# A hybrid diffusion step on one core: an eighth slot for expert weights, and attention queries scaled by ScalarE

## The chip, the cores and the metric

One NeuronCore of a Trainium2 chip runs the whole program. Its engines work side by side and wait for each other through semaphores: TensorE (PE) multiplies matrices into PSUM banks, VectorE (DVE) and ScalarE (ACT) read them out, GpSimd (POOL) helps with elementwise work, and SyncE (SP) issues most of the DMA transfers that bring weights from HBM into SBUF. The metric is the time of one execution in microseconds (us); a kernel is given by the median of its runs.

## The reference

Two layers act on 384 tokens of width 1024 (128 context tokens, 256 latent tokens). Everything is 32-bit. Each layer:

```
h   = rms_norm(x) * (1 + scale1) + shift1          # scale, shift, gate: from the conditioning vector
A   = grouped-query attention, 8 heads of 64, q and k RMS-normalised per head, rotary positions
B   = latent attention, 8 heads of 64 + 32, low-rank keys and values
C   = bidirectional gated linear recurrence (chunk scan)
x  += gate1 * ((sum over A, B, C of sigmoid(g_n) * (branch_n @ w_branch_n)) @ w_out)
h   = rms_norm(x) * (1 + scale2) + shift2
x  += gate2 * moe(h)                                # 16 experts, 2 per token, width 512
```

Attention is `softmax(q @ k.T * scale) @ v`, with `scale = 64 ** -0.5` in A and `96 ** -0.5` in B. Each expert has three weight matrices of 2 MB: gate, up and down.

## The kernel before, in words

**Slabs.** All large weights come as slabs of 128 x 4096 floats (2 MB). `slab_order()` lists them in the order in which they are loaded; `slab_slots()` gives each one a place. There are four ring slots (`sb_slabs`, slots 0 to 3) for everything, and three extra slots (slots 4 to 6, a part of `sb_arena` that the mixers no longer need at the end of a layer) for expert slabs alone. A slab takes the slot whose old slab is done with first. SP walks through the list: for each slab it waits until the slot's old slab has been read, then issues the load (L2088). The queue is in order, so a waiting load holds up all that follow. The slabs `eg`, `eu` and `ed` are an expert's gate, up and down matrices; `m` slabs are parts of the conditioning matrix, `o0` and `o1` the output projection, `br2` the third branch's projection.

**The mixer part of a layer.** PE computes the projections slab by slab. Attention runs over 24 units per layer: 2 mixers x 4 pairs of heads x 3 query tiles. The first tile of a pair sees 128 keys, the other two see 384. Per unit and head, `scores` (PE, L982) fills a bank, `maxima` (DVE) takes the row maximum negated (L1816) and multiplies it by the scale (L1817), `exps` (ACT, L1539) takes exp(scale * score - max) with its row sum, `softmax` (DVE, L1824 and L1826) divides, `turn` (PE, L1224) transposes, `probs_turned` (ACT, L1549) copies to SBUF, `values` (PE, L1241) multiplies by v, and `outputs` (DVE, L1832) copies the result to `oBr`, the branch outputs. PE's order is scores of unit s, turn of unit s - 1, values of unit s - 2. The queries come out of PSUM by ACT copies in `split` (mixer A, which also takes the squares for the head norm) and at L1512 (mixer B). After attention come the recurrence, the merge of the three branches (the last merge matmuls carry the key `("p", l, 2, j)`), the output projection, the second norm and the routing.

**The experts.** With at most 64 tokens per expert, the short path runs (`pe_short`, `act_short`, `dve_short`). Experts go in 8 pairs. For pair p, PE gathers the tokens by a matmul with a 0/1 matrix `pick` (L531), computes gate and up (L560, 32 matmuls each, one slab per expert and matrix), transposes (L570), and computes down of the pair before (L589). DVE tells SP by the semaphores `read_eg`, `read_eu` and `read_ed` (L754) when a pair's slabs have been read: two slots come free at a time. The rows of pairs 0 to 5 go through `yg` and an indirect DMA of GpSimd (L2059) to a buffer in HBM, `ybuf`; when all have landed, ACT's queue reads the buffer back in three parts (L691), ACT and DVE add a token's two rows (L697, L820), and PE transposes the sum back (L641). Pairs 6 and 7 are added by matmuls (L611). The down matmuls of pair 7 come after that transpose in PE's order.

`arena` holds, one after the other, the norm's scratch and `hT` (the normalised tokens, offsets 0 to 4224), the branch outputs `oBr` (from `o0` = 4224, 4608 long) and a region. During the experts, `hg`, `actT` and `ag` lie over the first part, `yg` and `pick` over the branch outputs. `tmp` (3072 long) holds squares and scratch of the norms and is free during the short expert path.

Of the kernel before, what the change touches and what calls it, by code (L numbers as in the profile page):

```python
# [27 lines left out]
D = 1024  # L28
# [29 lines left out]
RING = 4  # L58
EXTRA = 3
EXTRA_AT = 6144  # L60
GATES = 2
# [56 lines left out]
def slab_slots(order):  # L118

    index = {(l, n): i for i, (l, n, _) in enumerate(order)}
    ends = [index[l, f"g{n[2]}1"] if n[:2] == "br" else
            index[l, EXPERT_SLABS[EXTRA]] - 1 + (EXPERT_SLABS.index(n) + 1) / NE if n in AHEAD.values() else i for i, (l, n, _) in enumerate(order)]
    holds, times, out = [None] * (RING + EXTRA), [0] * (RING + EXTRA), []
    for i in range(len(order)):
        s = min(range(RING + EXTRA if order[i][1][0] == "e" else RING), key=lambda s: -1 if holds[s] is None else ends[holds[s]])
        times[s] += 1
        out.append((s, times[s], holds[s]))  # L130
        holds[s] = i
    return out
# [20 lines left out]
def program(nc, A, known):  # L153
# [5 lines left out]
    with ExitStack() as ctx:  # L159
# [14 lines left out]
        def signal(name, key):  # L174

            tally.next(name, key)
            return sem(name), 1
# [159 lines left out]
        hg = arena[:, 0:KT * 2 * SLOTS].rearrange("p (k n) -> p k n", k=KT)  # L337
        actT = arena[:, 2048:2048 + FT * 2 * SLOTS].rearrange("p (f n) -> p f n", f=FT)
        ag = arena[:, 3072:3072 + FE]
        yg = arena[:, o0:o0 + 2 * D].rearrange("p (b d) -> p b d", b=2)  # L340
        pick = arena[:, o0 + 2 * D:o0 + 2 * D + 3 * TT * 2 * SLOTS].rearrange("p (b t n) -> p b t n", b=3, t=TT)
        back = arena[:, KT * 2 * SLOTS:KT * 2 * SLOTS + 2 * T].rearrange("p (b t) -> p b t", b=2)
        extra = region[:, EXTRA_AT:EXTRA_AT + EXTRA * SLAB].rearrange("p (s n) -> p s n", s=EXTRA)
        ybuf = [nc.dram_tensor(f"ybuf{l}", (2 * T, D), F32).ap() for l in range(DEPTH)]

# [8 lines left out]
        dma_ytok = [[sem(f"dma_ytok{l}{t}") for t in range(TT)] for l in range(DEPTH)]  # L354
        dma_slab = [sem(f"dma_slab{i}") for i in range(RING + EXTRA)]
        outs = [0]

        def place(slot):
            return slabs[:, slot, :] if slot < RING else extra[:, slot - RING, :]

# [1061 lines left out]
        def _(sc):  # L1422
# [25 lines left out]

            def split(bkey, dst, sq, key, l, i, wait=None):

                sc.wait_ge(*full(bkey))
                ps = held(bkey)
                if wait:
                    wait()
                nc.scalar.activation(sq, ps[:, 0:T], ACT.Square).then_inc(*signal("square", (key, l, i)))
                nc.scalar.activation(dst, ps[:, 0:T], ACT.Copy).then_inc(*frees(bkey))

# [20 lines left out]
            for l in range(DEPTH):  # L1478
# [3 lines left out]
                for c in range(BT):  # L1482
                    split(("qa", l, c), qA[:, c, :], tmp[:, c, :], f"qa{c}", l, 0)
                for c in range(BT - 1):
# [24 lines left out]
                for h in range(HEADS):  # L1509
                    sc.wait_ge(*full(("qb", l, h)))  # L1510
                    ps = held(("qb", l, h))
                    nc.scalar.activation(qB[0:QB_W, h, :], ps[0:QB_W, 0:T], ACT.Copy).then_inc(*frees(("qb", l, h)))  # L1512
                if l == 0:
                    first_copy(NEXT + 1)
                for hp in range(HEADS // 2):
                    sc.wait_ge(*full(("kb", l, hp)))
                    ps = held(("kb", l, hp))
                    nc.scalar.activation(keysB[0:NOPE, 2 * hp, :], ps[0:HD, :], ACT.Copy).then_inc(*signal("kb_part", (l, hp)))
                    nc.scalar.activation(keysB[0:NOPE, 2 * hp + 1, :], ps[HD:P, :], ACT.Copy).then_inc(*frees(("kb", l, hp)))
# [7 lines left out]
                def exps(u):  # L1527
                    br, hp, qt = units[u]
                    c0, c1 = key_cols(qt)
                    for i in range(2):  # L1530
# [6 lines left out]
                        if u >= 2:  # L1537
                            sc.wait_ge(*full(("t", l, u - 2, i)))
                        nc.scalar.activation(probs[:, u % 2, i, 0:c1 - c0], ps[:, 0:c1 - c0], ACT.Exp, bias=nmx[:, u % 2, i:i + 1],  # L1539
                                                   scale=(SCALE_A, SCALE_B)[br], accum_out=rsum[:, u % 2, i:i + 1]).then_inc(*frees(("s", l, u, i)))  # L1540

# [120 lines left out]
        def _(ve):  # L1662
# [112 lines left out]
            for l in range(DEPTH):  # L1775
# [32 lines left out]
                def maxima(u):  # L1808
                    br, hp, qt = units[u]
                    c0, c1 = key_cols(qt)  # L1810
                    for i in range(2):
                        ve.wait_ge(*full(("s", l, u, i)))
                        ps = held(("s", l, u, i))
                        if u >= 2:
                            ve.wait_ge(*freed_by(("s", l, u - 2, i)))
                        step(V.tensor_reduce(nmx[:, u % 2, i:i + 1], ps[:, 0:c1 - c0], AX, ALU.max, negate=True))  # L1816
                        V.tensor_scalar(nmx[:, u % 2, i:i + 1], nmx[:, u % 2, i:i + 1], (SCALE_A, SCALE_B)[br], None, ALU.mult).then_inc(*signal("negmax", (l, u, i)))  # L1817

# [245 lines left out]
        def _(sp):  # L2064
# [3 lines left out]
            for i, (l, name, size) in enumerate(order):  # L2068
# [15 lines left out]
                if name == EXPERT_SLABS[EXTRA - 1]:  # L2084
                    sp.wait_ge(dma_out, 16 * (5 * l + 5))
                if l and i == index_of[l, "kv"] + 1:
                    sp.wait_ge(*made("x_ready", (l, 1, KT - 1)))
# [163 lines left out]
```

## Time and profile before

| what | value |
|---|---|
| median of 3 runs | 1878.6 us (1877.42 to 1880.3) |
| profiled execution: its time, its span | 1875.93 us, 1874.0 us |
| PE busy in the span | 1696.2 us (91%) |
| DVE, ACT, POOL busy | 945.3, 358.9, 353.7 us |
| mean granted TensorE clock | 0.955 |
| moved by DMA | 361.53 MB |

The span runs from the first to the last instruction that the profiler saw. Busy shares are averages over stages with different limits: a stage is read by the wait that ends last in it. The experts of layer 0 run from about 704 to 958 us, those of layer 1 from about 1606 to 1862 us; the attention units run from about 156 to 225 us and from about 1066 to 1136 us.

### The profile page before, as it was taken

The numbers are of one execution on the slowest core, as the hardware profiler recorded it, in microseconds if no ns is written. First come the engines' busy times: TensorE is split into PE (matmuls) and PEld (weight loads), VectorE is DVE, ScalarE is ACT, GpSimd is POOL, SyncE is SP. The second block draws the span as 40 slices with busy tenths as digits, with TensorE's granted clock in tenths as the row PEclk, the third lists the DMA queues.
The fourth block names the chain that finished last, engine by engine and source line by source line (L and its number), as shares of the span: only waits on it lengthen the run. The fifth ranks groups of instructions, "written<-read, shape, count | busy, mean of one in ns | idle before, by whom it ended". The sixth has DMA issues, their size and how long they took to land. (4 is left out here: it accounts for less than half of the span.)

```text
span 1874.0 us, 24758 instructions
## 1 busy us (share of the span) xinstructions
PE 1696.2 (91%) x9810; PEld 973.5 (52%) x9810; DVE 945.3 (50%) x2096; ACT 358.9 (19%) x827; POOL 353.7 (19%) x456
## 2 busy tenths in 40 slices
PE   4998999899889979998879999998998999899986
PEld 2554655555556645454346455655655555554443
DVE  0546658968855640010255585788776653210114
ACT  2125510110020031110112462110101102211102
POOL 0000108708700000000000001573573000000000
PEclk8999999999989989999989999998998999899998
DMA  9424032041045427999942300411413443399993
GB/s 377 164 97 181 7 143 98 8 194 76 25 186 224 198 117 298 419 428 426 428 191 70 138 2 29 180 46 68 180 46 151 181 196 152 146 408 428 428 428 155
DMA packets 30507, 361.53 MB, mean 193 GB/s; under 512 B 4296, under 2 KB 5672, under 8 KB 7728
## 3 DMA queue, kind: packets, MB, share of 16 engines
q1 hardware_dynamic: 26416, 341.42, 44.7%
q0 software_dynamic: 3104, 12.13, 1.7%
q10 hardware_dynamic: 864, 6.29, 0.8%
q8 instruction: 83, 1.36, 0.3%
q14 instruction: 40, 0.33, 0.1%
HBM read 352.55 MB, written 15.24 MB: 196 GB/s over the span
## 5 line engine op out<-in xcount | busy, mean ns | idle before, releaser
L982 PE MATMUL bank<-sb_arena,sb_slabs 128*128 128x384 f32 (+3 forms) x2016 | 706.1, 508 | 5.1 <-ACT sb_arena L1621 5.1
L982 PEld LDWEIGHTS bank<-sb_arena,sb_slabs 128*128 128x128 f32 (+2 forms) x2016 | 385.4, 195 | 280.0 <-issue 64.8
L560 PE MATMUL bank<-sb_arena 128*64 128x512 f32 x512 | 159.0, 613 | 11.1 <-DMA sb_arena<-in_W 7.3
L1703 DVE SCALAR_TENSOR_TENSOR sb_arena<-sb_slabs,sb_cv,sb_arena 128x512 f32<-128x512 f32 x238 | 159.1, 745 | 0.0
L2059 POOL DMA_INDIRECT ybuf<-sb_arena,sb_idx x12 | 11.8, 987 | 761.6 <-ACT sb_arena L683 761.6
L560 PE MATMUL bank<-sb_slabs,sb_arena 128*64 128x512 f32 x512 | 154.2, 593 | 0.1
L1679 DVE RECIPROCAL sb_arena<-sb_arena 128x384 f32<-128x384 f32 x22 | 56.1, 2550 | 92.1 <-ACT sb_arena L1446 92.1
L531 PEld LDWEIGHTS bank<-sb_arena 128*128 128x128 f32 x768 | 91.0, 199 | 18.0 <-issue 11.4
L531 PE MATMUL bank<-sb_arena 128*128 128x128 f32 x768 | 94.0, 284 | 6.4 <-DVE sb_arena L735 6.4
L560 PEld LDWEIGHTS bank<-sb_arena 128*64 128x64 f32 x512 | 50.3, 141 | 91.2 <-issue 91.2
L589 PE MATMUL bank<-sb_slabs,sb_arena 128*64 128x512 f32 x352 | 86.2, 602 | 1.8 <-issue 1.8
L982 PE MATMUL bank<-sb_tmp,sb_slabs 128*128 128x384 f32 x256 | 84.0, 488 | 2.6 <-issue 2.6
L560 PEld LDWEIGHTS bank<-sb_slabs,sb_arena 128*64 128x64 f32 x512 | 48.4, 137 | 61.2 <-issue 61.2
L427 POOL TENSOR_TENSOR sb_arena<-sb_arena 64x256 f32<-64x256 f32 x84 | 77.9, 928 | 0.0
L762 DVE TENSOR_TENSOR sb_arena<-sb_arena,bank 128x512 f32<-128x512 f32 x16 | 11.0, 687 | 124.3 <-PE bank L560 124.3
L427 DVE TENSOR_TENSOR sb_arena<-sb_arena 64x256 f32<-64x256 f32 x84 | 70.7, 841 | 0.0
L426 POOL TENSOR_TENSOR sb_arena<-sb_arena 64x256 f32<-64x256 f32 x84 | 68.6, 817 | 6.6
L430 DVE TENSOR_TENSOR sb_arena<-sb_arena 64x256 f32<-64x256 f32 x84 | 67.0, 798 | 2.9
L429 DVE TENSOR_TENSOR sb_arena<-sb_arena 64x256 f32<-64x256 f32 x84 | 65.8, 783 | 2.9
L982 PEld LDWEIGHTS bank<-sb_tmp,sb_slabs 128*128 128x128 f32 x256 | 48.2, 190 | 36.1 <-issue 3.8
L429 POOL TENSOR_TENSOR sb_arena<-sb_arena 64x256 f32<-64x256 f32 x84 | 64.4, 767 | 6.6
L430 POOL TENSOR_TENSOR sb_arena<-sb_arena 64x256 f32<-64x256 f32 x84 | 59.3, 706 | 6.6
(238 smaller groups left out, 1941.0 us busy)
## 6 DMA issues: line engine op xcount, KB each, us to landing
sb_slabs<-in_W SPq DMA_DIRECT2D x114, 2048.0 KB, 13.5
sb_arena<-in_W SPq DMA_DIRECT2D x42, 2048.0 KB, 17.5
ybuf<-in_W POOLq DMA_DIRECT2D x6, 1024.0 KB, 13.2
sb_slabs<-in_W SPq DMA_DIRECT2D x6, 1024.0 KB, 7.6
sb_arena<-ybuf ACTq DMA_DIRECT2D x6, 1024.0 KB, 18.9
sb_slabs<-in_W SPq DMA_DIRECT2D x2, 1152.0 KB, 10.1
sb_xT<-in_xT SPq DMA_DIRECT2D x1, 1536.0 KB, 22.5
out_y<-sb_arena SPq DMA_DIRECT2D x2, 768.0 KB, 3.3
```

What stands on the lines that cost most here:

```text
L426: E.tensor_tensor(halves(Ql[n][r], qs), halves(qd[r, :, cols], qs), halves(Pp[r], qs), ALU.mult)
L427: E.tensor_tensor(halves(Kl[n][r], ks), halves(Kg[r, :, cols], ks), halves(Rr[r], ks), ALU.mult).then_inc(*signal(f"lev_{tag}", (l, hh, tt ...
L429: step(E.tensor_tensor(halves(Rr[r], ks), halves(Rr[r], ks), halves(Pp[r], qs, edge), ALU.mult))
L430: step(E.tensor_tensor(halves(Pp[r], qs), halves(Pp[r], qs), halves(Pp[r], ks, edge), ALU.mult))
L531: mm = nc.tensor.matmul(ps[:, i * P:(i + 1) * P], lhsT=htok[:, t, c * P:(c + 1) * P], rhs=pick[:, p % 3, t, :], start=(t == 0), stop=(t == ...
L560: mm = nc.tensor.matmul(ps[half, :], lhsT=hg[:, k, half], rhs=w[i][:, k, :], start=(k == 0), stop=(k == KT - 1))
L589: mm = nc.tensor.matmul(ps[n][half, :], lhsT=actT[:, f, half], rhs=w[i][:, f, n * 512:(n + 1) * 512], start=(f == 0), stop=(f == FT - 1))
L762: V.tensor_tensor(ag[:, :], ag[:, :], held(key)[:, :], ALU.mult).then_inc(*frees(key))
L982: mm = nc.tensor.matmul(out, lhsT=w, rhs=a, start=(i == 0), stop=(i == n - 1))
L1679: step(V.reciprocal(std[:, s, :], std[:, s, :]))
L1703: ins = V.scalar_tensor_tensor(sums[:, g, 0:n], w[:, k, 0:n], cv[:, 2 * k + g:2 * k + g + 1], sums[:, g, 0:n], ALU.mult, ALU.add)
L2059: po.indirect_dma_start(ybuf[l], bass.IndirectOffsetOnAxis(ap=idx[:, p:p + 1], axis=0), yg[:, p % 2, :], None, bounds_check=2 * T - 1, oob ...
```

## The change

A slot 7 is added for expert slabs. It lies over the branch outputs, at `o0`, and is 4096 long. `yg` and `pick` move out of its way: `yg` into `tmp`, `pick` into the space of `hT`, where `actT` and `ag` move closer together. The first four expert slabs of a layer (`eg0`, `eg1`, `eu0`, `eu1`) are placed by name into slots 4 to 7; before its load of `eu1`, SP waits until the last merge matmul of the third branch has read the branch outputs.

In attention, the factor `scale` moves from the scores to the queries: the ACT copies that take the queries out of PSUM carry it as an immediate, `exps` drops it, and DVE's multiplication of the maximum (L1817, with the wait before it) goes. A signal that nothing waited for (`kb_part`) goes too.

```diff
+SLOTS_W = RING + EXTRA + 1
...
-    holds, times, out = [None] * (RING + EXTRA), [0] * (RING + EXTRA), []
+    holds, times, out = [None] * SLOTS_W, [0] * SLOTS_W, []
     for i in range(len(order)):
-        s = min(range(RING + EXTRA if order[i][1][0] == "e" else RING), key=lambda s: -1 if holds[s] is None else ends[holds[s]])
+        name = order[i][1]
+        s = min(range(SLOTS_W if name[0] == "e" else RING), key=lambda s: -1 if holds[s] is None else ends[holds[s]])
+        if name in EXPERT_SLABS[:EXTRA + 1]:
+            s = RING + EXPERT_SLABS.index(name)
...
-        actT = arena[:, 2048:2048 + FT * 2 * SLOTS].rearrange("p (f n) -> p f n", f=FT)
-        ag = arena[:, 3072:3072 + FE]
-        yg = arena[:, o0:o0 + 2 * D].rearrange("p (b d) -> p b d", b=2)
-        pick = arena[:, o0 + 2 * D:o0 + 2 * D + 3 * TT * 2 * SLOTS].rearrange("p (b t n) -> p b t n", b=3, t=TT)
+        actT = arena[:, 1792:1792 + FT * 2 * SLOTS].rearrange("p (f n) -> p f n", f=FT)
+        ag = arena[:, 2304:2304 + FE]
+        yg = tmp[:, :, :].rearrange("p a t -> p (a t)")[:, D:3 * D].rearrange("p (b d) -> p b d", b=2)
+        pick = arena[:, 2816:2816 + 3 * TT * 2 * SLOTS].rearrange("p (b t n) -> p b t n", b=3, t=TT)
...
+        last_slot = arena[:, o0:o0 + SLAB]
...
-                nc.scalar.activation(dst, ps[:, 0:T], ACT.Copy).then_inc(*frees(bkey))
+                nc.scalar.activation(dst, ps[:, 0:T], ACT.Copy, scale=scale).then_inc(*frees(bkey))
...
-                    split(("qa", l, c), qA[:, c, :], tmp[:, c, :], f"qa{c}", l, 0)
+                    split(("qa", l, c), qA[:, c, :], tmp[:, c, :], f"qa{c}", l, 0, SCALE_A)
...
-                    nc.scalar.activation(qB[0:QB_W, h, :], ps[0:QB_W, 0:T], ACT.Copy).then_inc(*frees(("qb", l, h)))
+                    nc.scalar.activation(qB[0:QB_W, h, :], ps[0:QB_W, 0:T], ACT.Copy, scale=SCALE_B).then_inc(*frees(("qb", l, h)))
...
-                                                   scale=(SCALE_A, SCALE_B)[br], accum_out=rsum[:, u % 2, i:i + 1]).then_inc(*frees(("s", l, u, i)))
+                                                   accum_out=rsum[:, u % 2, i:i + 1]).then_inc(*frees(("s", l, u, i)))
...
-                        step(V.tensor_reduce(nmx[:, u % 2, i:i + 1], ps[:, 0:c1 - c0], AX, ALU.max, negate=True))
-                        V.tensor_scalar(nmx[:, u % 2, i:i + 1], nmx[:, u % 2, i:i + 1], (SCALE_A, SCALE_B)[br], None, ALU.mult).then_inc(*signal("negmax", (l, u, i)))
+                        V.tensor_reduce(nmx[:, u % 2, i:i + 1], ps[:, 0:c1 - c0], AX, ALU.max, negate=True).then_inc(*signal("negmax", (l, u, i)))
...
+                if name == EXPERT_SLABS[EXTRA]:
+                    sp.wait_ge(*full(("p", l, 2, KT - 1)))
```

The order of SP's queue at the start of layer 0's experts, before. The first row is the load of `o1`; `sb_slabs` are ring slots, `sb_arena` the extra ones, and the brackets name the semaphore that a load waits for (`bank_full`: a matmul group that reads the slot's old slab; `mod_partial`: a DVE sum that does).

```order
L2088 DMA sb_slabs<-in_W 128x4096 [waits bank_full2]
L2088 DMA sb_slabs<-in_W 128x4096 [waits mod_partial]
L2088 DMA sb_slabs<-in_W 128x4096 [waits bank_full0]
L2088 DMA sb_slabs<-in_W 128x4096 [waits mod_partial]
L2088 DMA sb_slabs<-in_W 128x4096 [waits bank_full5]
L2088 DMA sb_slabs<-in_W 128x4096 [waits mod_partial]
L2088 DMA sb_arena<-in_W 128x4096 [waits read_eg] x2
L2088 DMA sb_arena<-in_W 128x4096 [waits read_eu]
L2088 DMA sb_slabs<-in_W 128x4096 [waits read_eu]
```

The same place of SP's queue after the change.

```order
L2092 DMA sb_slabs<-in_W 128x4096 [waits bank_full2]
L2092 DMA sb_slabs<-in_W 128x4096 [waits mod_partial]
L2092 DMA sb_arena<-in_W 128x4096 [waits bank_full3]
L2092 DMA sb_slabs<-in_W 128x4096 [waits bank_full0]
L2092 DMA sb_slabs<-in_W 128x4096 [waits mod_partial]
L2092 DMA sb_slabs<-in_W 128x4096 [waits bank_full5]
L2092 DMA sb_slabs<-in_W 128x4096 [waits mod_partial]
L2092 DMA sb_arena<-in_W 128x4096 [waits read_eg] x2
L2092 DMA sb_arena<-in_W 128x4096 [waits read_eu] x2
```

The list of slabs is the same, but `eu1` now goes to slot 7, after the third branch's last merge; `eg2`, `eg3`, `eu2` and `eu3` take the four ring slots that `eu1`, `eg2`, `eg3` and `eu2` took before. So `eu3` no longer waits for `read_eg`, and each later slab waits for the slab that is eight places before it instead of seven.

At the other end of the experts, the next layer's first slab, `qa`, took the slot of `ed13` before and takes that of `eu14` now.

DVE's rows of one attention unit, before: one query tile with 384 keys in mixer A.

```order
L1816 TENSOR_REDUCE sb_arena<-bank 128x1 [waits bank_free1,bank_full3]
L1817 TENSOR_SCALAR sb_arena<-sb_arena 128x1 [waits dve_step]
L1816 TENSOR_REDUCE sb_arena<-bank 128x1 [waits bank_free2,bank_full4]
L1817 TENSOR_SCALAR sb_arena<-sb_arena 128x1 [waits dve_step]
L1824 RECIPROCAL sb_arena<-sb_arena 128x1 [waits bank_free3]
L1826 TENSOR_SCALAR sb_tmp<-sb_tmp,sb_arena 128x384 [waits dve_step]
L1824 RECIPROCAL sb_arena<-sb_arena 128x1 [waits bank_free4]
L1826 TENSOR_SCALAR sb_tmp<-sb_tmp,sb_arena 128x384 [waits dve_step]
```

And after the change, the same unit.

```order
L1819 TENSOR_REDUCE sb_arena<-bank 128x1 [waits bank_free1,bank_full3]
L1819 TENSOR_REDUCE sb_arena<-bank 128x1 [waits bank_free2,bank_full4]
L1826 RECIPROCAL sb_arena<-sb_arena 128x1 [waits bank_free3]
L1828 TENSOR_SCALAR sb_tmp<-sb_tmp,sb_arena 128x384 [waits dve_step]
L1826 RECIPROCAL sb_arena<-sb_arena 128x1 [waits bank_free4]
L1828 TENSOR_SCALAR sb_tmp<-sb_tmp,sb_arena 128x384 [waits dve_step]
```

Two small multiplications with their waits are gone from each unit, 96 in the whole program; the rest stands as it was. PE and POOL run the same instructions in the same order, and so does ACT.

## Rows read from the trace of the kernel before

**Rows 1.** Stages (us): busy PE, PEld, DVE, ACT, POOL (count), PEclk, DMA share, GB/s.

```profile
714.00:942.00 228.00, 212.62 (x1147) 103.82 (x1144) 31.82 (x125) 27.00 (x49) 5.92 (x6) 0.97 1.00 419
1622.00:1842.00 220.00, 209.10 (x1125) 99.33 (x1120) 27.81 (x118) 25.72 (x48) 5.93 (x6) 0.98 0.99 416
870.00:880.00 10.00, 6.20 (x26) 2.04 (x24) 0.06 (x1) 0.60 (x1) 0.00 (x0) 0.85 1.02 433
1780.00:1790.00 10.00, 6.53 (x22) 1.95 (x20) 0.06 (x1) 0.60 (x1) 0.00 (x0) 0.74 1.00 426
```

**Rows 2.** Waits of PE, layer 0's experts: total us, times, longest.

```profile
PE bank L560 <- DMA sb_arena<-in_W: 3.8, 1, 3.8
PE bank L560 <- DMA sb_slabs<-in_W: 1.2, 1, 1.2
```

**Rows 3.** Waits of PE, layer 1's experts.

```profile
PE bank L641 <- DVE sb_arena L820: 3.7, 2, 3.1
...
PE bank L560 <- DMA sb_arena<-in_W: 3.5, 1, 3.5
...
PE bank L560 <- DMA sb_slabs<-in_W: 2.3, 1, 2.3
```

**Rows 4.** Chain that ended last, layer 1's experts: start us, us, what.

```profile
1755.31 7.10 PE bank L560 x32
...
1763.17 22.74 DMA sb_arena<-in_W
...
1786.05 9.88 PE bank L560 x32
...
1822.62 21.14 DMA sb_arena<-ybuf
...
1846.37 1.09 PE bank L641 x8
1847.46 7.04 PE bank L589 x32
```

**Rows 5.** The load of eu12, layer 1 (the slab before eu13): issue, time to landing.

```profile
L2088 SPq DMA_DIRECT2D sb_arena<-in_W x1: 432/432/432, 1753.5 to 1753.5; - x1
...
DMA to landing us min/median/max: 26.6/26.6/26.6
```

**Rows 6.** The three reads of ybuf, layer 0: first and last issue, time to landing.

```profile
L691 ACTq DMA_DIRECT2D sb_arena<-ybuf x3: 348/449/453, 911.3 to 912.2; - x3
...
DMA to landing us min/median/max: 11.3/19.2/26.1
```

**Rows 7.** PE in order of time, end of layer 0's experts.

```profile
940.94 1.97 PE L641 MATMUL bank<-sb_con,sb_arena 128*128 128x128 f32 x8 [4.82 <-DVE sb_arena L820]
942.84 8.24 PE L589 MATMUL bank<-sb_slabs,sb_arena 128*64 128x512 f32 x32
```

**Rows 8.** Two units of mixer B in order of time (layer 0): start, us, engine, instruction, idle before.

```profile
201.89 1.56 PE L982 MATMUL bank<-sb_arena 96*128 96x384 f32 x4
...
202.95 0.55 DVE L1816 TENSOR_REDUCE sb_arena<-bank 128x1 f32<-128x384 f32 x1
...
203.54 0.15 DVE L1817 TENSOR_SCALAR sb_arena<-sb_arena 128x1 f32<-128x1 f32 x1
...
203.73 0.58 ACT L1539 ACTIVATE sb_tmp<-bank,sb_arena 128x384 f32<-128x384 f32 x1 [1.21 <-DVE sb_arena L1817]
...
205.30 0.42 DVE L1826 TENSOR_SCALAR sb_tmp<-sb_tmp,sb_arena 128x384 f32<-128x384 f32 x1
...
207.39 1.56 PE L982 MATMUL bank<-sb_arena 96*128 96x384 f32 x4
...
208.34 0.56 DVE L1816 TENSOR_REDUCE sb_arena<-bank 128x1 f32<-128x384 f32 x1 [0.42 <-PE bank L982]
```

**Rows 9.** Scores of a unit with 384 keys, mixer A.

```profile
174.29 0.92 PE L982 MATMUL bank<-sb_arena 64*128 64x384 f32 x4
```

**Rows 10.** ACT's table loads at the exponentials: busy us, mean ns.

```profile
L1539 ACT ACT_TABLE_LOAD x2 | 2.6, 1283 | 0.0
```

More of the change, by code:

```diff
@@ L354, in program @@
         dma_ytok = [[sem(f"dma_ytok{l}{t}") for t in range(TT)] for l in range(DEPTH)]
-        dma_slab = [sem(f"dma_slab{i}") for i in range(RING + EXTRA)]
+        dma_slab = [sem(f"dma_slab{i}") for i in range(SLOTS_W)]
         outs = [0]
         def place(slot):
-            return slabs[:, slot, :] if slot < RING else extra[:, slot - RING, :]
+            return slabs[:, slot, :] if slot < RING else extra[:, slot - RING, :] if slot < RING + EXTRA else last_slot
         def W(l, name):
@@ L1447, in root, with split @@
                 nroot[0] += 1
-            def split(bkey, dst, sq, key, l, i, wait=None):
+            def split(bkey, dst, sq, key, l, i, scale=1.0):
                 sc.wait_ge(*full(bkey))
                 ps = held(bkey)
-                if wait:
-                    wait()
                 nc.scalar.activation(sq, ps[:, 0:T], ACT.Square).then_inc(*signal("square", (key, l, i)))
-                nc.scalar.activation(dst, ps[:, 0:T], ACT.Copy).then_inc(*frees(bkey))
+                nc.scalar.activation(dst, ps[:, 0:T], ACT.Copy, scale=scale).then_inc(*frees(bkey))
             def first_copy(i):
@@ L1517, in _ @@
                     ps = held(("kb", l, hp))
-                    nc.scalar.activation(keysB[0:NOPE, 2 * hp, :], ps[0:HD, :], ACT.Copy).then_inc(*signal("kb_part", (l, hp)))
+                    nc.scalar.activation(keysB[0:NOPE, 2 * hp, :], ps[0:HD, :], ACT.Copy)
                     nc.scalar.activation(keysB[0:NOPE, 2 * hp + 1, :], ps[HD:P, :], ACT.Copy).then_inc(*frees(("kb", l, hp)))
```

## The prediction

> **What bounds the kernel now.** I read the stages first, then the waits of PE in the stages that the change touches, then the chain of waits at the end, and last single units of attention in order of time. Two kinds of stage matter.
>
> In the experts, the 16 DMA engines have no room: their share is 1.00 and 0.99 over 228 and 220 us, at 419 and 416 GB/s [rows 1]. PE is nearly always busy there too. It waits for expert weights only twice per layer, 1.2 + 3.8 = 5.0 us in layer 0 [rows 2] and 2.3 + 3.5 = 5.8 us in layer 1 [rows 3]: for seven slabs it lives on what was loaded ahead, and for pairs 5 and 6 the stock has run out. The last of these waits costs more than itself. In layer 1 PE starts the up matmuls of pair 6 when `eu13` lands, at 1763.17 + 22.74 = 1785.9, and they take 9.88 us where the same 32 matmuls took 7.10 before [rows 4]; the granted clock of that stretch is 0.74 [rows 1], so part of it ran at the lower of its two levels. The reader should see a DMA-bound stage whose debt is paid late, and an end that hangs on one transfer: the last of the three reads of `ybuf` (21.14 us), after which come the sum, the transpose and the down matmuls of pair 7 [rows 4].
>
> In attention, DVE and PE hand work to each other. A unit with 384 keys is a DVE-ACT chain; behind the second such unit of a pair of heads PE becomes the one that is late, and DVE idles 0.42 us [rows 8].
>
> **The change part by part.**
>
> *The eighth slot.* The load of `eu1` moves to slot 7, and one more slab, `eu3`, is in SBUF before the experts begin. Its wait (third branch merged) costs nothing: `m11` and `m2`, ahead of it in SP's queue, already wait for that same matmul through `br2`'s slot. Behind it stand `eg2` to `eu3`, which take the places of `eu1` to `eu2`, on the same releases.
>
> From there the two queues can be laid side by side. The first slots come free when pair 0's gates are read, an event of PE that does not move. Every event frees two slots, as before. So as long as PE runs as before, the same number of bytes is outstanding at every moment, and the n-th transfer lands when the n-th landed, but it is one slab further down the list. Each slab lands when its predecessor did. For `eu13` of layer 1 that is `eu12`'s time: 1753.5 + 26.6 = 1780.1 instead of 1785.9 [rows 4, 5], 5.8 us earlier. PE would be ready at 1786.05 - 5.8 = 1780.2. Both waits disappear, and the fall of the clock with them: 5.8 + (9.88 - 7.10) = 8.6 us at this point. In layer 0 likewise 5.0 us of waits, plus 0.15 of 10 us of clock [rows 1], 6.5 us.
>
> What is late next is the read of `ybuf`. Its issue follows PE's chain, so it comes 8.6 and 6.5 us earlier; its landing depends on the bytes that share the DMA engines.
> - Layer 1: from the first release to the end of the read the engines are full, and the total is less by one slab. 2.097 MB at 416 GB/s [rows 1] is 5.0 us: the read cannot end more than that earlier, whatever PE does. So 5.0 of the 8.6.
> - Layer 0: the same queue goes on into layer 1's `qa` and `kv`, so the weights keep the engines full through the whole read, which took 26.1 us from its last issue [rows 6] against 21.1 in layer 1 [rows 4]. With weights still queued all the time it takes the 26.1 again, from an issue 6.5 us earlier: 6.5. The bounds are 5.0 (one slab) and 10 (two slabs, since `qa` now waits for `eu14` and is issued during the read and no longer before it). I take 6.5, the row's own duration.
>
> One cost comes with it. In layer 1 PE can now finish its other work up to 8.6 us earlier, while the read ends only 5.0 earlier: the last of PE's two waits for the sums, 3.7 - 3.1 = 0.6 us [rows 3], grows by up to 3.6. In layer 0 that wait is 4.82 us, and what follows ran slow: 1.97 and 8.24 us for the transposes and the down matmuls [rows 7] against 1.09 and 7.04 [rows 4], 2.1 us in all. Between the two rows I take half, 1.0 us (bounds 0 and 2.1). The Trainium skill, page "TensorE: Matmul & The Clock Gate", section "HAM oscillation — how this bites in real kernels", says that waits for data put the array back to its slow clock, so that the next piece of work starts cold. The trace agrees in both places above; by the rule in full, layer 1 would give back the whole 2.1.
>
> So the slot gives 6.5 in layer 0 and 5.0 - 1.0 = 4.0 in layer 1. `yg` in `tmp` and `pick` in `hT` carry no new wait: `tmp` is idle then, and `pick` is written after the routing's flag, which itself waits for matmuls behind the transposes that read `hT`. I cost both at nothing; if that cover were gone, the six small comparisons that fill `pick` would stand on the path, once per layer.
>
> *Attention.* 96 multiplications of 0.15 us go [rows 8], two in each of 48 units, with a wait in front of each. Only the first of a unit lies on the chain: the second is hidden behind the first exponential. In a 384-key unit the first exponential starts 0.78 us after the reduction (202.95 to 203.73); the reduction takes 0.55, and the step from DVE to ACT 0.04 (203.69 to 203.73) [rows 8], so 0.59 is left: 0.19 less. There are 16 such units per layer, in 8 groups of two. The 128-key unit gains nothing: the next unit's scores start after turn and values on PE, 205.72 to 208.34, and DVE already waits for them [rows 8].
> - Mixer A: both heads' scores together take 0.92 us [rows 9] and are there in time, so a group gains 2 x 0.19 = 0.38; four groups, 1.5 us.
> - Mixer B: scores start at 201.89 and take 1.56 for both heads; in the later unit DVE could start its first reduction 0.95 after PE did (207.39 to 208.34) [rows 8]. The same lag after 201.89 gives 202.84, so DVE can start only 0.11 earlier than 202.95, and its second reduction waits for the second head. I get about 0.25 per group; four groups, 1.0 us.
>
> That is 2.5 us per layer, 5.0 in all. The bounds are 0 (PE sets every unit) and 96 x 0.19 = 18.2 (each removed one on the chain). The scaled copies of the queries I cost at nothing: same instructions, same count, an immediate other than 1.
>
> **Sum.** 6.5 + 4.0 + 5.0 = 15.5 us. From the profiled execution's 1875.9 that gives 1860.4; the median of the runs stands 2.7 above that execution, so 1863.1, and I predict 1863.
>
> **The rivals.**
> 1. *Attention's gain is not seen* (PE is the bound in every unit). For it: behind the 128-key unit DVE waits for PE's scores already, 0.42 us. Against it: in front of the other 384-key unit (202.95) it does not [rows 8]. Then 10.5 us are left: 1868.
> 2. *The slot buys only attention's part.* The slab comes earlier, but the read of `ybuf` ends no earlier, because the weights that are queued ahead of it share the engines as before. For it: the end hangs on that read in both layers. Against it: the bytes are fewer. Then 5 us are left: 1873.6.
> 3. *All removed multiplications count.* If DVE sets every unit, 18.2 + 10.5 = 28.7: 1850. Against it: PE is waited for at 208.34 [rows 8].
> 4. *Slower: a scaled copy needs another table on ACT.* A load of a table takes 1.283 us [rows 10]; 4 + 8 scaled copies per layer stand among squares and roots, 24 in all, at least one load each, 30.8 us. From 12 loads on the path they eat the 15.5; all of them give 1863 + 31 = 1894. Against it: the plain copies of the queries stand at the same places between the same functions, and only a factor changes.
>
> **How the numbers follow.** The forecast, with each term within its bounds by a third or so (1858 to 1868), 0.62. Rival 1: 0.14. Rival 2: 0.08. Rival 3: 0.08. Rival 4: 0.03. Something else, both ways: 0.05. The range from 1857 to 1870 holds the forecast and rival 1, with some 0.2 outside. Below 0.2% (3.8 us) a measurement of this kernel cannot tell a change from none. Faster than that: the forecast and rivals 1 to 3, 0.92, and a little of the rest. Same: 0.05. Slower: 0.03.
>
> **What would show it.** In the changed profile PE's waits for weights in the experts' up matmuls (L560) of pairs 5 and 6 are gone or under 1 us each, and the stretch of pair 6 in layer 1 runs at a clock of 1.00; PE's wait before the last transposes of layer 1 (L641) has grown from 0.6 us to 2 or more. The DMA share in the experts stays at 0.99 or 1.00. Three units of attention take 0.38 us (A) and 0.25 us (B) less, and DVE's wait for scores behind the 128-key unit is there still. If the waits are gone and the time is not, rival 2 holds; if there are table loads on ACT beyond those of before, rival 4. The prediction is wrong if the stages between attention and the experts take up the 2.5 us per layer, or if the experts' DMA share falls.

## The result and the profile after

The changed kernel takes 1855.6 us, the median of 4 runs (1851.93 to 1858.05), against 1879.45 (4 runs, 1877.42 to 1882.36). The ratio is 0.9869, 95% interval [0.9849, 0.9888]. Forecast were 1863 us and a range of 1857 to 1870: the direction was right, the gain too small: 15.5 us by its sum (which ended at 1863.1) against 23.9, and the time lies 7.5 us below that sum. The profiled execution took 1856.75 us (span 1854.8, mean granted clock 0.958), 19.2 us less than that of before.

The stages of [rows 1], the windows moved with the start of the stage (the first two) or of pair 6's up matmuls; columns as there.

```profile
711.10:937.10 226.00, 216.66 (x1166) 105.01 (x1164) 36.85 (x143) 26.84 (x49) 5.93 (x6) 0.97 0.99 414
1605.30:1825.30 220.00, 209.49 (x1140) 101.93 (x1136) 30.45 (x119) 26.84 (x49) 5.95 (x6) 0.99 0.97 407
868.70:878.70 10.00, 10.00 (x60) 5.11 (x57) 0.76 (x3) 0.60 (x1) 0.00 (x0) 1.00 1.02 432
1765.20:1775.20 10.00, 9.98 (x58) 5.60 (x59) 0.70 (x2) 0.00 (x0) 0.00 (x0) 1.00 1.00 424
```

The share of 0.97 in layer 1 is that of a window as long as before around a stage that has become shorter: the last read now lands in it, at 1822.9. Without its two ends (before, after):

```profile
1628.00:1840.00 212.00, 203.10 (x1097) 96.91 (x1093) 26.88 (x116) 23.12 (x46) 5.93 (x6) 0.98 1.00 422
1611.00:1820.00 209.00, 200.68 (x1099) 96.79 (x1096) 28.46 (x118) 25.19 (x47) 5.95 (x6) 1.00 1.00 420
```

So the DMA engines are as full as before, while the clock of pair 6's stretch has gone from 0.85 and 0.74 to 1.00. The waits of PE, layer 0's experts, to be held against [rows 2]:

```profile
PE bank L646 <- DVE sb_arena L825: 6.3, 2, 3.2
...
PE bank L565 <- DMA sb_slabs<-in_W: 0.6, 1, 0.6
```

And layer 1's, against [rows 3]:

```profile
PE bank L646 <- DVE sb_arena L825: 5.6, 2, 3.1
PE bank L565 <- DMA sb_slabs<-in_W: 2.8, 2, 2.1
```

In layer 0 the 5.0 us of waits for weights have become 0.6; in layer 1 5.8 have become 2.8, of which 2.1 stand before the up matmuls of pair 6 and 0.7 before those of pair 7, which did not wait before. The second wait for the sums in layer 1 has grown from 0.6 to 5.6 - 3.1 = 2.5 us. The chain that ended last, layer 1's experts (start us, us, what), against [rows 4]:

```profile
1729.09 7.04 PE bank L565 x32
1736.64 28.44 DMA sb_slabs<-in_W
1765.22 7.09 PE bank L565 x32
...
1798.74 24.19 DMA sb_arena<-ybuf
...
1825.55 1.54 PE bank L646 x8
1827.09 8.24 PE bank L594 x32
```

The up matmuls of pair 6 take 7.09 us instead of 9.88. The read of `ybuf` is issued at 1798.74 instead of 1822.62, and takes 24.19 us instead of 21.14. In layer 0 its last part took 25.2 instead of 26.1 [rows 6]:

```profile
L696 ACTq DMA_DIRECT2D sb_arena<-ybuf x3: 348/451/454, 901.4 to 902.3; - x3
...
DMA to landing us min/median/max: 11.3/18.3/25.2
```

Before, the changed kernel and its halves run the same 9810 matmuls in the same order, so that a stage can be cut at the start of the same matmul in each. The table has the stages of every profile taken of before, of the changed kernel and of its halves, in us, with the time at the lower clock (1.2 GHz) in brackets. In the first profile of before the stages end at 82.8, 276.1 (attention, from 159.5), 713.4, 940.9, 1053.7, 1189.3, 1621.4 and 1846.4 us. "To sums" ends where the last eight transposes of the sums start (L641 before, L646 after), "end" runs from there to the end of the span.

| stage | before, three profiles | changed, three profiles | slot alone | queries alone, two |
|---|---|---|---|---|
| start | 82.8, 85.7, 83.2 | 85.2, 83.1, 83.7 | 83.7 | 83.4, 85.2 |
| attention 0 | 116.62 (3.4), 116.81 (3.4), 116.56 (3.4) | 113.48 (3.4), 113.48 (3.4), 114.29 (5.4) | 116.84 (3.4) | 113.42, 113.50 |
| recurrence, merge 0 | 437.33, 435.27, 434.99 | 435.02, 435.04, 434.31 | 435.31 | 434.78, 435.03 |
| experts 0, to sums | 227.50, 227.18, 227.07 | 219.70, 219.98, 219.61 | 219.71 | 228.30, 229.06 |
| to layer 1's scores | 112.72 (7.7), 110.30 (4.4), 110.28 (4.6) | 110.70 (5.1), 110.42 (4.9), 110.53 (5.2) | 110.88 | 112.00, 111.18 |
| attention 1 | 135.66 (3.4), 138.39 (10.2), 136.90 (6.8) | 132.23 (3.4), 132.23 (3.4), 133.90 (6.8) | 136.87 (6.8) | 132.37 (3.4), 132.38 (3.4) |
| recurrence, merge 1 | 432.08, 431.97, 433.21 | 431.57, 431.57, 433.35 | 433.18 | 431.74, 431.80 |
| experts 1, to sums | 224.97, 225.65, 224.79 | 221.01, 220.58, 219.99 | 219.56 | 225.11, 226.22 |
| end | 27.61, 27.60, 29.47 | 29.26, 29.50, 27.61 | 27.61 | 27.61, 30.26 |

Four stages differ by more than they scatter, the two attentions and the two experts, and they are the ones that the forecast named. By the means the changed kernel's span is 20.3 us shorter. Not in the table are 76.6 to 77.0 us between the first two stages, nearly the same in all.

### The profile page after: what moved, and what is told of

It is laid out like the page before. It is cut to its first block and busy times, and to the rows that moved or that the text cites. A ratio compares the mean times of both kernels' runs of the same rounds, so it can differ in the third digit from the quotient of the medians.

```text
span 1854.8 us, 24663 instructions
## 1 busy us (share of the span) xinstructions
PE 1692.5 (91%) x9810; PEld 971.9 (52%) x9810; DVE 932.2 (50%) x2000; ACT 356.3 (19%) x827; POOL 354.7 (19%) x456
## 5 line engine op out<-in xcount | busy, mean ns | idle before, releaser
L2061 POOL DMA_INDIRECT ybuf<-sb_tmp,sb_idx x12 | 11.9, 990 | 747.4 <-ACT sb_arena L688 747.4
L565 PE MATMUL bank<-sb_slabs,sb_arena 128*64 128x512 f32 x512 | 112.4, 594 | 3.4 <-DMA sb_slabs<-in_W 3.4
L565 PE MATMUL bank<-sb_arena 128*64 128x512 f32 x512 | 112.4, 594 | 0.3 <-issue 0.3
L536 PEld LDWEIGHTS bank<-sb_arena 128*128 128x128 f32 x768 | 90.9, 199 | 18.1 <-issue 11.4
L565 PEld LDWEIGHTS bank<-sb_slabs,sb_arena 128*64 128x64 f32 x512 | 37.3, 137 | 73.7 <-issue 73.7
L565 PEld LDWEIGHTS bank<-sb_arena 128*64 128x64 f32 x512 | 37.7, 137 | 68.2 <-issue 68.2
L594 PE MATMUL bank<-sb_slabs,sb_arena 128*64 128x512 f32 x256 | 59.5, 619 | 0.0
```

The lines of the kernel that those rows point to most:

```text
L536: mm = nc.tensor.matmul(ps[:, i * P:(i + 1) * P], lhsT=htok[:, t, c * P:(c + 1) * P], rhs=pick[:, p % 3, t, :], start=(t == 0), stop=(t == ...
L565: mm = nc.tensor.matmul(ps[half, :], lhsT=hg[:, k, half], rhs=w[i][:, k, :], start=(k == 0), stop=(k == KT - 1))
L594: mm = nc.tensor.matmul(ps[n][half, :], lhsT=actT[:, f, half], rhs=w[i][:, f, n * 512:(n + 1) * 512], start=(f == 0), stop=(f == FT - 1))
L2061: po.indirect_dma_start(ybuf[l], bass.IndirectOffsetOnAxis(ap=idx[:, p:p + 1], axis=0), yg[:, p % 2, :], None, bounds_check=2 * T - 1, oob ...
```

## The experiments

**Which half is it?** Theory M: the mechanisms are as forecast and sized as the profile shows; theories S and A: the slot, or attention, is worth far more.

*The slot alone*: before, with everything of the change but the attention edits (three of the places).

```diff
+SLOTS_W = RING + EXTRA + 1
...
+        last_slot = arena[:, o0:o0 + SLAB]
...
+                if name == EXPERT_SLABS[EXTRA]:
+                    sp.wait_ge(*full(("p", l, 2, KT - 1)))
```

> The eighth slot and its moves alone; attention as before (scale on the scores, multiplication of the maximum kept). Theory M (the two mechanisms are sized as the changed kernel's profile shows them, experts 9.7 us, attention 6.5 us, and what is left of the 23.9 us is where slow-clock stretches happen to fall): 9 to 11 us below before, ratio about 0.9945. Theory S (the slot is the term that was mis-sized): 16 to 18 us below, ratio about 0.991. Theory A (attention is): about 10 us below, as M, and the attention-only kernel then 13 us below.

1867.17 us (10 runs), before 1880.09 (21 runs), ratio 0.9934 [0.9914, 0.9954]: 12.9 us. The stages give 7.5 in layer 0 and, with the end, 6.2 in layer 1 (225.14 + 28.23 by the means of before, less 219.56 + 27.61). Together 13.7 us. The time lies between M (9 to 11) and S (16 to 18), nearer to M; its interval, 8.6 to 16.2 us, leaves out neither for certain.

*The queries alone*: before, with the attention edits alone (two of the places).

```diff
-split(("qa", l, c), qA[:, c, :], tmp[:, c, :], f"qa{c}", l, 0)
+split(("qa", l, c), qA[:, c, :], tmp[:, c, :], f"qa{c}", l, 0, SCALE_A)
...
-                        V.tensor_scalar(nmx..., (SCALE_A, SCALE_B)[br], None, ALU.mult)
```

> The scaled queries alone; seven slots as before. Theory M: 6 to 7 us below before, ratio about 0.9965, a group of three units 0.59 us shorter in mixer A and 0.31 in mixer B. Theory S: 5 to 7 us below. Theory A: 12 to 14 us below, ratio about 0.993, with gains in stages behind attention too.

1869.98 us (12 runs), ratio 0.9955 [0.9938, 0.9971], which is 5.5 to 11.7 us. M's 6 to 7 lies inside and so does S's 5 to 7; A's 12 to 14 lies just outside. The medians alone do not tell M from S; the stages do. Both attention stages are shorter by as much as in the changed kernel. The halves add up: 12.9 + 10.1 = 23.0 us, against 23.4 for both in the next run.

*The changed kernel again*, unedited.

> The changed kernel once more, nothing edited. Theory M: its profile has the same 9.7 us in the experts and 6.5 us in attention within 1 us, but the stages that the change does not touch (start, recurrence and merge, start of layer 1) stand otherwise against before than in the first profile, by up to 3 us each, with slow-clock stretches at other places; the median lies within 1853 to 1859 us. Theories S and A: the same 2 to 3 us gains in the untouched stages come back, as a consequence of the change.

1856.66 us (6 runs), ratio 0.9884 [0.9854, 0.9913], 23.4 us. The four stages repeat within 0.5 us. The start moves by 2.1 us, as M expected; but the recurrence of layer 0 is again at 435.0, and so it is with either half alone, which M did not expect. If that gain is chance, the odd one is the first profile of before.

*Before again*, twice.

> The kernel before once more, unchanged, for a second profile of it. If the 2.2 us that all four later kernels gained between 440 and 514 us (13.7 us at the lower clock in the first profile of before, 10.2 in theirs) are chance, this profile has 10.2 us there and stands 1.5 to 2.2 us earlier at 714 us than the first. If they are a consequence of the change, it has 13.7 again and stands within 0.5 us, apart from the start.

> The kernel before, a third profile. Chance: recurrence and merge of layer 0 take 433 to 437.5 us and attention of layer 1 135.7 or 138.4 us, going with 3.4 or 10.2 us of lower clock in it; start 83 to 86 us. A consequence of the change: 437 us in the recurrence again.

435.27 and 434.99 us in that stage, and 10.2 us at the lower clock between 440 and 514 us in both, where the first profile had 13.7: chance, since the kernel is the same. The amount of lower clock alone is not what made the first one slow: over the whole stage it is 54.6 us in the first and in the second, 58.0 in the third. The first profile of before, on which the forecast stood, was 2.1 to 2.3 us slower there and 2.4 us in the stretch up to layer 1's scores than either of the later two; in layer 1's attention it was the fastest (the third took 136.90 us with 6.8 at the lower clock, neither of the two values expected). Their times were 1877.47 and 1875.05 us.

**Which multiplications lay on the chain?** The first in each unit only (theory F, the forecast's), or the second also (theory C)?

```diff
+if i == 0:            # the other kernel: i == 1
+    step(V.tensor_reduce(nmx..., ALU.max, negate=True))
+    V.tensor_scalar(nmx..., 1.0, None, ALU.mult).then_inc(*signal("negmax", (l, u, i)))
+else:
     V.tensor_reduce(nmx..., ALU.max, negate=True).then_inc(*signal("negmax", (l, u, i)))
```

> The changed kernel with a multiplication by 1.0 (and its wait) put back behind the maximum of the first head of each unit only; the second head's stays away. Theory F (as forecast: only the first head's multiplication lies on the chain): the whole gain of attention goes, a group of three units takes 8.27 us in mixers A and B as in the kernel before. Theory C (the second exponential starts when the later of two things is there, the first exponential's end and the second maximum; before, it was the maximum, 0.10 us later): a unit with 384 keys keeps 0.10 us, a group in mixer A takes 8.05 to 8.10 us.

> The same with the multiplication by 1.0 put back behind the second head's maximum only. Theory F: nothing changes, 7.68 us per group in mixer A and 7.96 in mixer B. Theory C: the second maximum is there 0.05 to 0.10 us after the first exponential has ended, so a unit with 384 keys loses 0.05 to 0.10 us, a group in mixer A takes 7.8 to 7.9 us.

One profile of each, 1859.57 us with the first kept and 1860.58 with the second. A group of three units in mixer A takes 8.27 us in before, 8.06 with the first kept, 7.86 with the second kept, 7.68 changed. Theory F said 8.27 and 7.68 for the middle two: it falls. C said 8.05 to 8.10 and 7.8 to 7.9. In mixer B the four are 8.27, 8.07, 8.15 and 7.96: F's 8.27 and 7.96 fall there too, and for C no number had been given. Taking away the first multiplication alone gains 8.27 - 8.15 = 0.12 us there, the second alone 0.20. The same unit with 384 keys of mixer A, DVE's rows in before (start, us, instruction):

```profile
175.24 0.56 DVE L1816 TENSOR_REDUCE sb_arena<-bank 128x1 f32<-128x384 f32 x1 [0.42 <-PE bank L982]
175.83 0.15 DVE L1817 TENSOR_SCALAR sb_arena<-sb_arena 128x1 f32<-128x1 f32 x1
175.91 0.56 DVE L1816 TENSOR_REDUCE sb_arena<-bank 128x1 f32<-128x384 f32 x1
176.50 0.15 DVE L1817 TENSOR_SCALAR sb_arena<-sb_arena 128x1 f32<-128x1 f32 x1
```

ACT's rows in before:

```profile
176.02 0.58 ACT L1539 ACTIVATE sb_tmp<-bank,sb_arena 128x384 f32<-128x384 f32 x1 [1.15 <-DVE sb_arena L1817]
176.50 0.19 ACT L1539 ACTIVATION_READ_ACCUMULATOR sb_tmp<-bank,sb_arena 128x1 f32 x1
176.69 0.58 ACT L1539 ACTIVATE sb_tmp<-bank,sb_arena 128x384 f32<-128x384 f32 x1
```

DVE's in the changed kernel, the two reductions in one row:

```profile
176.87 1.02 DVE L1819 TENSOR_REDUCE sb_arena<-bank 128x1 f32<-128x384 f32 x2 [0.55 <-PE bank L987]
178.17 0.16 DVE L1826 RECIPROCAL sb_arena<-sb_arena 128x1 f32<-128x1 f32 x1 [0.28 <-ACT sb_tmp L1542]
```

ACT's in the changed kernel:

```profile
177.47 0.58 ACT L1542 ACTIVATE sb_tmp<-bank,sb_arena 128x384 f32<-128x384 f32 x1 [1.21 <-DVE sb_arena L1819]
177.95 0.19 ACT L1542 ACTIVATION_READ_ACCUMULATOR sb_tmp<-bank,sb_arena 128x1 f32 x1
178.04 0.57 ACT L1542 ACTIVATE sb_tmp<-bank,sb_arena 128x384 f32<-128x384 f32 x1
```

With the first multiplication kept, DVE and then the exponentials:

```profile
176.78 0.56 DVE L1820 TENSOR_REDUCE sb_arena<-bank 128x1 f32<-128x384 f32 x1 [0.42 <-PE bank L987]
177.37 0.15 DVE L1821 TENSOR_SCALAR sb_arena<-sb_arena 128x1 f32<-128x1 f32 x1
177.45 0.56 DVE L1823 TENSOR_REDUCE sb_arena<-bank 128x1 f32<-128x384 f32 x1
```

```profile
177.56 0.58 ACT L1542 ACTIVATE sb_tmp<-bank,sb_arena 128x384 f32<-128x384 f32 x1 [1.21 <-DVE sb_arena L1821]
...
178.13 0.57 ACT L1542 ACTIVATE sb_tmp<-bank,sb_arena 128x384 f32<-128x384 f32 x1
```

And with the second kept:

```profile
176.91 0.56 DVE L1823 TENSOR_REDUCE sb_arena<-bank 128x1 f32<-128x384 f32 x1 [0.55 <-PE bank L987]
177.39 0.55 DVE L1820 TENSOR_REDUCE sb_arena<-bank 128x1 f32<-128x384 f32 x1
177.97 0.15 DVE L1821 TENSOR_SCALAR sb_arena<-sb_arena 128x1 f32<-128x1 f32 x1
```

```profile
177.51 0.58 ACT L1542 ACTIVATE sb_tmp<-bank,sb_arena 128x384 f32<-128x384 f32 x1 [1.18 <-DVE sb_arena L1823]
...
178.16 0.58 ACT L1542 ACTIVATE sb_tmp<-bank,sb_arena 128x384 f32<-128x384 f32 x1
```

In before, the second exponential starts at 176.69, just behind the second multiplication (176.50 + 0.15) and 0.67 after the first exponential's start; in the changed kernel it follows the first back to back, after 0.57. From the first reduction to the second exponential it is 1.45 us in before, 178.13 - 176.78 = 1.35 with the first kept, 178.16 - 176.91 = 1.25 with the second kept, 1.17 changed. The unit takes 2.89, 2.78, 2.68 and 2.60 us: always 1.43 to 1.44 more. What sets such a unit in mixer A is the second exponential. What sets one in mixer B is not shown.

**Do weights that could wait slow the read of `ybuf`?** The last slab, `ed15`, is held back until the read has landed. As written this serves the short expert path alone, the one that these inputs take: the general path issues no such read.

```diff
+if name == EXPERT_SLABS[-1]:
+    for t in range(TT):
+        sp.wait_ge(dma_ytok[l][t], 16)
 sp.dma_start(place(slot)[:, 0:size], A["W"][i, :, 0:size]).then_inc(dma_slab[slot], 16)
```

> The changed kernel, but the load of a layer's last slab, ed15, is issued only when all three parts of the read of ybuf have landed. If the read is late because the queued weights share the engines' bytes, the third part lands about 5 us (one slab) earlier, the wait before the last transposes shrinks from 2.4 us to under 1, and the last matmuls wait for ed15 at about the time when the read landed: 2 to 4 us faster per layer than the changed kernel, 1848 to 1852 us. If the read runs at its own pace whatever else is queued, it lands when it did, ed15 lands 5 to 8 us behind it, and the kernel is 2 to 5 us slower per layer, 1860 to 1866 us.

1851.76 us (6 runs, 1849.73 to 1855.0), ratio 0.9855 [0.9827, 0.9884], against 1856.66 for the changed kernel beside it: the lowest median of all, as the first of the two theories had it. The read in layer 1:

```profile
L696 ACTq DMA_DIRECT2D sb_arena<-ybuf x3: 332/450/452, 1792.6 to 1793.4; - x3
...
DMA to landing us min/median/max: 11.5/18.5/20.3
```

PE at the end of layer 1's experts:

```profile
1815.70 4.39 PE L646 MATMUL bank<-sb_con,sb_arena 128*128 128x128 f32 x24 [3.11 <-DVE sb_arena L825]
1821.40 7.09 PE L594 MATMUL bank<-sb_slabs,sb_arena 128*64 128x512 f32 x32 [1.30 <-DMA sb_slabs<-in_W]
```

The last part lands after 20.3 us instead of 24.2, the 24 transposes run without a second wait, and PE waits 1.3 us for `ed15` in its place. In layer 0 it lands after 19.8 us instead of 25.2. Up to the sums the stages take 216.55 and 218.16 us, against means of 219.76 and 220.53 in the changed kernel; in layer 0 the lower clock is down too, from 8.5 to 8.8 us to 2.0. So the read was late by the weights that shared the engines with it.

**Can more be had from the end?** The reads go on SP's queue behind `ed15`, PE does pair 7's down matmuls before the transposes, and pair 7's rows are copied out before the last sum. PE's part of the edit:

```diff
 turn(PAIRS - 1)
+down(PAIRS - 1)
 for t in range(TT):
     pe.wait_ge(*made("ysum" + W_, t))
...
-down(PAIRS - 1)
 add_back(PAIRS - 1)
```

> The changed kernel with three things reordered at the end of the experts: the three reads of ybuf are issued on SP's queue behind the load of ed15 instead of on ACT's queue; PE does the down matmuls of pair 7 before the transposes of the sums; ACT and DVE copy out pair 7's rows before the last of the three sums. If the end of a layer is bound by bytes that share the engines, the weights drain first, the down matmuls run while the read still lands, and behind its end stand only a scale, a sum, eight transposes and the last 16 matmuls: 5 us per layer less than with ed15 held back, 1840 to 1846 us. If what stands behind the read sets the end, or if the weights come no earlier, the time is that of the kernel with ed15 held back, 1850 to 1853 us, or worse.

1852.26 us (4 runs, 1850.75 to 1855.85): no better than `ed15` held back. DVE at the end of layer 1:

```profile
1825.54 6.29 DVE L831 SCALAR_TENSOR_TENSOR sb_xT<-bank,sb_mod,sb_xT 128x128 f32<-128x128 f32 x24
1831.74 5.28 DVE L798 SCALAR_TENSOR_TENSOR sb_xT<-bank,sb_mod,sb_xT 128x128 f32<-128x128 f32 x16
```

And PE, waiting for it:

```profile
1837.08 2.79 PE L990 MATMUL bank<-sb_tmp,sb_con 128*32 128x96 f32 x64 [4.29 <-DVE sb_xT L798]
```

The order of the matmuls is another here, so the table's cut at the last transposes does not serve; the stages on both sides of it can be compared together. From the start of the experts to layer 1's scores, layer 0 takes 330.3 us, as in the changed kernel (330.1 to 330.4), where `ed15` held back takes 326.8; from the experts of layer 1 to the end it is 245.6 us, against 247.6 to 250.3 and 247.3. DVE's 24 additions, which lay beside the down matmuls, now stand in a row with the other 16, and PE waits 4.29 us for them, where it waited 0.87 in the changed kernel. To take the 24 additions away, PE then added the sums onto pair 7's rows in PSUM:

```diff
+                for t in range(TT if p > SENT else 0):
+                    pe.wait_ge(*made("ysum" + W_, t))
+                    for j in range(KT):
+                        ps = held(("yb", l, p, j))
+                        mm = nc.tensor.matmul(ps[:, t * P:(t + 1) * P], lhsT=ytok[:, t, 0, j * P:(j + 1) * P], rhs=con[:, IDN:IDN + P], start=False, stop=t == TT - 1)
...
```

> The reordered kernel once more, with one step less behind the last read: PE adds the sums onto pair 7's rows in the same eight PSUM banks (24 matmuls with the identity instead of 24 transposes into banks of their own), so that DVE's 24 additions of 128x128 go (6.29 us in the reordered kernel's profile, with its 16 other additions, 5.28 us, behind them). If DVE's additions are what the reordering gave its gain back to, 4 to 6 us per layer less than the reordered kernel: 1841 to 1846 us. If PE or the clock sets that stretch (2.79 us for the norm's 64 matmuls that take 1.57 at full clock), 1849 to 1853 us.

1854.93 us (5 runs, 1849.73 to 1855.16). This lies in neither range: DVE's 16 additions start at 1831.99, no earlier than 1831.74 (1.6 us later, if both are counted from the start of layer 1's experts), since PE's added matmuls with the identity (L623, 5.52 us) end late; they have taken the place of the additions.

**Is the slow end a consequence?** Two more profiles, of the queries alone and of the changed kernel.

> The scaled queries alone, a second profile. Its medians said 9 us, its first profile 3.2 us per layer in the attention stages. If the rest lies in stages that the edit does not touch and is chance, the two stages gain 3.2 again and the others scatter by 1 to 3 us either way with the slow-clock stretches in them. If it is a consequence, the recurrence of layer 0 stands again 2.5 us below the first profile of before and the start of layer 1 0.7 us below.

> The changed kernel, a third profile. Both theories: attention 113.5 and 132.2 us, experts of layer 0 to the last transposes 219.7 to 220.0 us, of layer 1 220.1 to 221.0 us. By chance, the last transposes and last down matmuls of layer 1 run at full clock this time (1.50 and 15.34 us, as in the kernel with the slot alone); by a consequence of the longer last wait, they take 1.6 to 2.4 and 16.1 to 16.9 us again.

The queries alone took 1873.21 us this time. The attention stages repeat (113.50 and 132.38 us). The recurrence of layer 0 took 435.03 us, 2.3 below the first profile of before, which by the expectation would make it a consequence; but before itself takes 435.0 to 435.3 in its later profiles, so it is not one. The changed kernel's attention did not come out as expected: 114.29 and 133.90 us, with 5.4 and 6.8 at the lower clock. PE at the end of layer 1 in the third profile of the changed kernel:

```profile
1826.67 1.10 PE L646 MATMUL bank<-sb_con,sb_arena 128*128 128x128 f32 x8 [2.45 <-DVE sb_arena L825]
1827.69 7.09 PE L594 MATMUL bank<-sb_slabs,sb_arena 128*64 128x512 f32 x32
```

The same in the third profile of before:

```profile
1843.64 1.97 PE L641 MATMUL bank<-sb_con,sb_arena 128*128 128x128 f32 x8 [1.73 <-DVE sb_arena L820]
1845.53 8.07 PE L589 MATMUL bank<-sb_slabs,sb_arena 128*64 128x512 f32 x32
```

A wait of 2.45 us with full speed behind it, and one of 1.73 with the slow clock behind it, in a kernel without the slot. So the slow end is no sure consequence. That it comes more often with both edits is not ruled out: the end is slow in four of the five profiles of the changed kernel and of the two with one multiplication put back (30.23 and 30.09 us there), and in two of the six of before and the halves.

## Why the prediction missed

**The steps that failed.** By the forecast the profiled execution would take 1860.4 us and the median 2.7 more. The three profiled executions of the changed kernel take 1855.8 in the mean, and its median is 1855.6. Of the 7.5 us missing, 4.6 are in the forecast of the execution and 2.9 in the step from there to the median.

- *Attention, 5.0.* It measures 6.6 with 3.4 us at the lower clock in each: 116.66 - 113.48 = 3.2 and 135.66 - 132.23 = 3.4. The step that failed is "the second is hidden behind the first exponential". In mixer A it was hidden but for 0.10 us in each unit with 384 keys: two heads' chains meet on ACT, and I had followed the first alone. A group gains 0.59 there instead of 0.38, of which 8.27 - 7.86 = 0.41 are the first multiplication's, as forecast. In mixer B it is 0.31 instead of 0.25, and that the forecast came near is luck: the first one alone gains 0.12, the second, which had been put at nothing, the rest. The rest of that step held: the unit with 128 keys takes 2.50 us before and after, and DVE's wait behind it is there still (0.55).
- *Slot, layer 0, 6.5.* Mean 7.5 (227.25 to 219.76). "It takes the 26.1 again" was the mis-sized term: the read took 25.2 (25.6 to 26.3 in the three profiles of before, 25.2 to 25.4 in the changed kernel's). `qa` is issued at 919.36, 17 us after the read's last part, where it used to be issued 3.6 us ahead of it (908.58); I had named this in the bounds and given it nothing. That it is what shortened the read is likely, but not shown.
- *Slot, layer 1, 5.0 - 1.0.* The 5.0 measured 4.6 (225.14 to 220.53). "Both waits disappear" was too much: the stage starts 16.9 us earlier than before, yet `eu13` landed only 15.0 us ahead of `eu12`'s time, and pair 6 still waits 2.1, pair 7 another 0.7. In the three profiles these waits sum to 2.8, 2.5 and 1.9 us. They cost 0.4 us at most, if the one slab's 5.0 was right. The 1.0 for the end is not shown: full speed and slow clock come in both kernels, 27.6 or 29.3 to 30.3 us, and the means differ by 0.6. So 4.6 - 0.6 = 4.0, the forecast's own number, is met by two terms that were both too large, which is luck. The last wait did grow to 2.5, as said. By the rule cited from the Trainium skill ("TensorE: Matmul & The Clock Gate", "HAM oscillation — how this bites in real kernels"), taken for every wait, all 2.1 us would have been given back each time. The traces agree in part: the end is 1.6 to 1.9 us longer in two of the three profiles and at full speed in the third. The section tells of long waits that come again and again, which this one is not.
- *The profile it stood on.* The terms now sum to 6.6 + 7.5 + 4.6 - 0.6 = 18.1 us, 2.6 over the forecast. From 1875.9 that gives 1857.8. The 2.0 left to 1855.8 lie mostly in stages that the change does not touch: the first profile of before was 2.1 to 2.4 us slower than its successors in each of two, and other stages took part of that back.
- *"The median of the runs stands 2.7 above that execution."* For before this holds (medians of 1878.5 to 1880.3 against 1875.9, 1877.5 and 1875.1), for the changed kernel it doesn't (1855.6 and 1856.7 against 1856.75, 1854.43 and 1856.22). Its cause is not shown. Single runs of before go from 1871.3 to 1887.0, so three profiles that happened to be low are possible.

**What held.** Each slab landed when its predecessor had, within 0.6 us in layer 0 up to pair 6; in layer 1 it came up to 1.9 us later in the first profile, up to 0.6 in the third. The stretches of pair 6 run at a clock of 1.00. The scaled copies cost nothing, and ACT has the same 21 table loads (the rival of 1894). The slot buys more than attention (against the rival of 1873.6). The rival of 1850, all 96 multiplications on the chain, came nearer to the time than the forecast, yet not by its mechanism: 6.6 us and not 18.2.

**What stays open.** The sum of the terms is 18.1, the difference of the mean spans 20.3, that of the medians 23 to 24. The intervals of the halves hold the sums of their stages (13.7 in 8.6 to 16.2, 6.6 in 5.5 to 11.7); that of the first comparison (21 to 28) does not hold 18.1, that of the second (16 to 27) does.

## What to carry to other kernels

Where two chains meet on an engine, follow the one that arrives last: removing a step from both gains on the second as well. Cut the stages of two or three profiles at the same instructions before trusting a difference of 2 us; one profile of before can be unlucky in a stage that nobody touched. The cut holds only while the instructions keep their order. When a short read bounds the end and long loads share the engines with it, hold back a load that is needed later than the read.

## What had not been expected of the hardware

- Two reductions of 128x384 in a row on DVE, 0.56 us each, start 0.46 to 0.48 us apart and take 1.02 together; with the multiplication and its wait between them they started 0.67 apart. Removing an instruction of 0.15 us and its wait moves the next start by 0.2.
- On ACT's queue the first third of the read landed 11.3 us after its issue, while slabs issued up to 12 us before it were still in flight; on SP's queue behind `ed15` it took 21.1. The Trainium skill ("DMA: Bandwidth & Descriptors", "Issuing engines are not separate DMA queues") says that issuing from several engines saves only the time of the issue. Here, with the reads issued 11 to 12 us behind `ed15`'s load in both kernels, the queue also went with what landed first; the last third landed after 24.2 us on ACT's queue and 25.2 on SP's.
- The lower clock comes at similar places in each execution, but not at the same ones: the 6.8 us at 1283 us in before are 3.4 in the changed kernel's first profile, and layer 1's attention of before has 3.4, 10.2 or 6.8 us of it.
